# Three chunks of an input projection by seven half-size products instead of eight

## The chip, the core and the metric

The kernel runs on one core of one Trainium2 chip. The metric is device time in microseconds, the median of repeated executions. One further execution was profiled. In the profile the engines are PE (TensorE matmuls), PEld (TensorE weight loads), DVE (VectorE), ACT (ScalarE), POOL (GpSimd) and SP (the queue that issues most DMAs); a name like SPq is an engine's instruction queue.

## What is computed

One layer in float32 for 256 tokens of width 1024: RMSNorm, one input projection whose columns are split among the inputs of two token mixers, the mixers, an output projection with residual, and a mixture of 32 experts. Cut to what matters:

```python
h = rms_norm(x, norm1_gain[layer])
proj = jnp.einsum('bsd,dn->bsn', h, w_in[layer])
q_a, k_a, v_a, q_i, k_i, w_i, q_b, k_b, v_b, g_b = jnp.split(proj, cuts, axis=-1)
...
out_a = dsa_attention(q_a, k_a, v_a, q_i, k_i, w_i, rel_bias, topk)   # indexer: relu(q_i k_i), weighted by w_i, top 64 keys
q_b = rotary(q_b.reshape(bsz, s, B_HEADS, B_QK_DIM), pos)
k_b = rotary(k_b.reshape(bsz, s, B_HEADS, B_QK_DIM), pos)
y_b = retention(q_b, k_b, v_b)
...
out_b = jax.nn.silu(g_b) * y_b
x = x + jnp.einsum('bsm,md->bsd', jnp.concatenate([out_a, out_b], -1), w_out[layer])
x = x + moe_ffn(rms_norm(x, norm2_gain[layer]), ...)                  # 32 experts, top 4
```

## The kernel before

The kernel is written for five engines by hand; each engine's block lists its instructions in order, and semaphores order the engines among each other. The normalised activations lie transposed in `hT`: 8 slices of 128 contraction rows by 256 tokens, not yet scaled by the tokens' inverse norms (`st[:, 6:8]`). The projection is worked in chunks of 512 columns, `C_QI, C_QKB, C_VB, C_GB, C_QA, C_KA, C_VA`, each a 1024 x 512 block of weights in one of four SBUF slots `win[0..3]`; SP loads the first four at the start and each later one when its slot is free (`load_win`, L251).

A chunk by token (`by_token`, `one_tile`, L1123 to L1132) takes, for each of two tiles of 128 tokens, 8 products of a 128x128 weight load with 512 moving columns, summed in one PSUM bank. `C_QKB` has the same products written out at L1193, with `index_scores` of the indexer put between them; `C_VB` and `C_GB` go through `chunk` (L1142). `C_QA` and `C_KA` go `by_head` (L1134), with 256 moving columns a product. A float32 product is two MATMUL records in the trace.

The order on TensorE around the change is: the index queries, `C_QKB` into banks 0 and 1 with four groups of index scores (banks 4 to 7), `C_VB` into banks 2 and 3, a wait for `rotated`, eight transposes of the rotated q and k (L1204), one product for the row of inverse norms (L1207), `C_GB` into banks 0 and 1, the retention scores (L1214, L1216) into banks 4 to 7, `C_QA`, the retention values, `C_KA`.

ScalarE takes the chunks out of PSUM and scales them by the inverse norms in the same instruction (L520 for q and k, L526 for the values), takes the relu of the index scores (L517), and the exponential of the gate (L540). VectorE adds the eight index heads into `score` (L770, L772; each an addition of two SBUF tensors with a factor), finds the top 64 keys by eight rounds of maxima and replacements (L781 to L788), splits the bias table into parts (L797, L799), finishes the gate (L807 to L809), and multiplies the retention scores by the decay (L814). GpSimd issues small table loads, multiplies q and k by the rotation table (`rot`, L459, four operations) and combines them (L463, L464), which releases `rotated`; later it loads the relative bias (L469, L470) and adds the mask (L476).

The relu of group 2 and 3 waits for `idx_added`, since `relu` has two buffers. The expert part begins behind the output projection and the router and streams 403 MB of expert weights (32 experts of 1024 x 2048 and 1024 x 1024 float32) through two SBUF rings; its loads are issued by SP as products free the rows.

Of the kernel before, what the change touches and what calls it, by code (L numbers as in the profile page):

```python
# [75 lines left out]
def hybrid_block(nc, x, norm1_gain, w_in, rel_bias, idx_k_ln_gain, idx_k_ln_bias, ret_gn_gain, w_out,  # L76
# [3 lines left out]
    with ctx:  # L80
# [24 lines left out]
        one_ready = sem("one_ready"); zeros_ready = sem("zeros_ready")  # L105
# [37 lines left out]
        va = carve(high, 5632, [TT, 512])  # L143

# [41 lines left out]
        x_in = [sem(f"x_in{t}") for t in range(TT)]; cols_sb = sem("cols_sb"); small_in = sem("small_in"); rel_in = sem("rel_in"); gain_in = sem("gain_in"); ln_in = sem("ln_in"); rot_in = sem("rot_in")  # L186
        wki_in = sem("wki_in"); dec_in = sem("dec_in"); br_in = sem("br_in"); gq_in = sem("gq_in"); rank_in = sem("rank_in"); wr_in = sem("wr_in"); late_consts = sem("late_consts")
# [17 lines left out]
        vb_sb = sem("vb_sb"); g_exp = sem("g_exp"); g_silu = sem("g_silu")  # L205
# [39 lines left out]
        C_QI, C_QKB, C_VB, C_GB, C_QA, C_KA, C_VA = range(7)  # L245
        CHUNK_COL = (1536, 2120, 2632, 3144, 0, 512, 1024)
# [187 lines left out]
        @block.gpsimd  # L434
        def _(pool):
            chain = [0]

            def link(ins):
                chain[0] += 1
                ins.then_inc(pool_chain, 1)  # L440
                pool.wait_ge(pool_chain, chain[0])


            for half in (slice(0, 64), slice(64, 128)):
                pool.dma_start(ln_rows[0:1, half], idx_k_ln_gain).then_inc(ln_in, 16)
                pool.dma_start(ln_rows[1:2, half], idx_k_ln_bias).then_inc(ln_in, 16)
            pool.dma_start(onehot[0:32, :], c_onehot).then_inc(rel_in, 16)
            pool.dma_start(relb[0:32, :], rel_bias).then_inc(rel_in, 16)
            pool.dma_start(rot, c_rot.rearrange("p (a t n) -> p a t n", a=2, t=TT)).then_inc(rot_in, 16)
            pool.wait_ge(win_in[C_QKB], 16)  # L450
            pool.dma_start(br[:, :], b_router.to_broadcast((P, NE))).then_inc(br_in, 16)
            pool.dma_start(gain_q, norm2_gain[0].rearrange("(c q j) -> q c j", c=2, q=P)).then_inc(gq_in, 16)
            pool.wait_ge(qkb_sb, 2)
            pool.wait_ge(rot_in, 16)
# [26 lines left out]
        def _(act):  # L481
# [7 lines left out]
            act.wait_ge(one_ready, 2)  # L489
# [219 lines left out]
        def _(dve):  # L709
# [9 lines left out]
            v.memset(zeros, 0.0).then_inc(zeros_ready, 1)  # L719
# [19 lines left out]
            ins.then_inc(diag_ready, 1)  # L739

# [16 lines left out]
            link(v.tensor_copy(cols[:, 20:22], ps[:, 4, 400:402]))  # L757

# [3 lines left out]
            v.tensor_scalar(kiT, ps[:, 5, 0:S], cols[:, LNG:LNG + 1], cols[:, LNB:LNB + 1], ALU.mult, ALU.add).then_inc(kiT_sb, 1)  # L762

# [11 lines left out]

            link(v.memset(score[0:64, P - CH:P], NEG))
# [27 lines left out]

            for t in range(TT):
# [3 lines left out]
                v.scalar_tensor_tensor(gb[:, t, :], ps[:, t, :], st[:, 6 + t:7 + t], gb[:, t, :], ALU.mult, ALU.mult).then_inc(g_silu, 1)  # L809

            dve.wait_ge(dec_in, 16)
            for h in range(BH):
                dve.wait_ge(ret_s, h // 2 + 1)
                v.tensor_tensor(sT[:, h, :], ps[:, 4 + h, 0:KW], dec[:, h, :], ALU.mult).then_inc(sT_sb, 1)  # L814
# [100 lines left out]
            dve.wait_ge(br_in, 16)  # L915
# [182 lines left out]
        def _(pe):  # L1098
# [3 lines left out]
            pe.wait_ge(zeros_ready, 1)  # L1102
# [26 lines left out]
            def by_token(w, bank, n):  # L1129
                for t in range(TT):  # L1130
                    ins = one_tile(w, bank, n, t)
                return ins  # L1132

# [8 lines left out]
            def chunk(c, banks, form):  # L1142
                pe.wait_ge(win_in[c % 4], 16 * (c // 4 + 1))
                ins = form(win[c % 4], banks) if form is by_head else form(win[c % 4], banks, 512)
                ins.then_inc(proj_done, 1)
# [8 lines left out]
            for k in range(KD):  # L1154
# [4 lines left out]
                if k == 3:  # L1159
                    pe.wait_ge(rel_in, 32)  # L1160
                    pe.wait_ge(ln_in, 64)
# [26 lines left out]

            pe.wait_ge(kiw_sb, 2)
            pe.wait_ge(win_in[C_QKB], 16)  # L1190
            for t in range(TT):
                for k in range(KD):
                    ins = mm(ps[:, t, :], hT[:, k, P * t:P * t + P], win[C_QKB][:, k, :], start=(k == 0), stop=(k == KD - 1))  # L1193
                    if k % 4 == 1:
                        index_scores(2 * t + k // 4)
            ins.then_inc(proj_done, 1)
            chunk(C_VB, 2, by_token)
            pe.wait_ge(rotated, 2)
            pe.wait_ge(idx_relu, 4)
            for which in range(2):  # L1200
                for g in range(2):
                    for t in range(TT):
                        at = 256 * which + 128 * g
                        ins = nc.tensor.transpose(ps[:, 4 + which, S * g + P * t:S * g + P * t + P], qkb[:, t, at:at + 128], ident)  # L1204
                ins.then_inc(qkbT_tr, 1)
            pe.wait_ge(diag_ready, 1)
            mm(ps[:, 6, 0:S], ones_early, diag.rearrange("p t n -> p (t n)"), start=True, stop=True).then_inc(row_mm, 1)  # L1207
            pe.wait_ge(qkb_sb, 2)
            chunk(C_GB, 0, by_token)
            pe.wait_ge(qkbT_sb, 2)  # L1210
            pe.wait_ge(row_sb, 1)
# [6 lines left out]
            pe.wait_ge(vb_sb, 2)  # L1218
# [9 lines left out]
            pe.wait_ge(g_silu, 2)  # L1228
# [404 lines left out]
```

## Time and profile before

| what | value |
| --- | --- |
| median of 3 runs | 1078.7 us (1077.63 to 1080.11) |
| the profiled execution | 1080.09 us |
| its span, first to last instruction | 1078.3 us |
| busy PE, DVE, ACT, POOL | 1040.4, 265.9, 152.9, 22.2 us |
| mean granted TensorE clock | 0.986 of 2.4 GHz |
| DMA | 429.87 MB, mean 399 GB/s |

The chain that ended last is followed back from the last instruction: at each step to what released it, or to the instruction before it on its engine. Granted clock is a share of 2.4 GHz, so 0.5 is the 1.2 GHz level. A DMA's time to landing runs from its issue. PE's records overlap, since matmuls are pipelined; in the chain they are cut to their own share of the time.

### The profile page before, as it was taken

How to read it: one execution, taken by the hardware profiler on the slowest of the kernel's cores; microseconds unless marked ns; L12 is line 12 of the kernel's file. 1: busy time of each engine (PE TensorE's matmuls, PEld its weight loads, DVE VectorE, ACT ScalarE, POOL GpSimd, SP SyncE). 2: the span in 40 equal slices, each digit the busy share in tenths (PEclk: the TensorE clock that was granted, in tenths of full speed). 3: DMA queues.
4: the chain of work that ended last, by engine and by line, in shares of the span. 5: the costliest groups of instructions: out<-in, count | busy, mean ns of one | idle time of the engine just before them, and what ended most of it. 6: DMA issues, size and time to landing. Idle time of an engine off the chain costs nothing.

```text
span 1078.3 us, 11417 instructions
## 1 busy us (share of the span) xinstructions
PE 1040.4 (96%) x4628; PEld 399.4 (37%) x4628; DVE 265.9 (25%) x649; ACT 152.9 (14%) x278; POOL 22.2 (2%) x29
## 2 busy tenths in 40 slices
PE   9999999999999999999999999898989899999996
PEld 7458454333333333333333333232323233333331
DVE  2455622422222222222220302121222212120221
ACT  1231322110111110101010111011101101111111
POOL 1212000000000000000000000000000000000000
PEclk9999998999999999999998999999999999999999
DMA  9886957999999999999999999999999999999996
GB/s 330 239 245 269 378 217 266 423 428 421 428 433 430 430 430 430 430 430 432 432 430 430 430 432 433 432 429 434 432 433 432 430 434 430 435 423 434 425 422 246
DMA packets 35376, 429.87 MB, mean 399 GB/s; under 512 B 5164, under 2 KB 6608, under 8 KB 16624
## 3 DMA queue, kind: packets, MB, share of 16 engines
q1 hardware_dynamic: 33424, 426.03, 93.8%
q10 hardware_dynamic: 1216, 1.70, 1.1%
q0 software_dynamic: 704, 1.71, 0.6%
q8 instruction: 21, 0.34, 0.1%
q14 instruction: 11, 0.09, 0.0%
HBM read 426.80 MB, written 2.62 MB: 398 GB/s over the span
## 4 chain that ended last, share of the span: by engine, by line
PE 72%; DMA 26%; SPq 0%; DVE 0%; issue 0%; ACT 0%; DVEq 0%
PE ps L1399 30%; DMA w1r<-w_mlp 24%; PE ps L1429 13%; PE ps L1467 5%; PE ps L1376 4%; PE ps L1126 3%; PE ps L1138 3%; DMA w2r<-w_mlp 2%; PE ps L1193 1%; PE ps L1257 1%; PE ps L1302 1%; PE ps L1158 1%; PE ps L1268 1%; PE ps L1383 1%; PE ps L1407 1%; PE ps L1443 1%
## 5 line engine op out<-in xcount | busy, mean ns | idle before, releaser
L1399 PE MATMUL ps<-w1r,arena 128*64 128x512 f32 x2024 | 478.0, 608 | 21.0 <-DMA w1r<-w_mlp 21.0
L1399 PEld LDWEIGHTS ps<-w1r,arena 128*64 128x64 f32 x2024 | 138.2, 139 | 281.7 <-issue 253.6
L1429 PE MATMUL ps<-w2r,arena 128*64 128x512 f32 x960 | 211.4, 593 | 6.6 <-DMA w2r<-w_mlp 6.6
L1429 PEld LDWEIGHTS ps<-w2r,arena 128*64 128x64 f32 x960 | 68.8, 137 | 145.1 <-issue 135.5
L964 DVE TENSOR_TENSOR arena<-ps,cols 128x512 f32<-128x512 f32 x31 | 21.4, 692 | 277.0 <-PE ps L1383 277.0
L1002 DVE TENSOR_TENSOR arena<-arena 128x512 f32<-128x512 f32 x32 | 22.1, 692 | 163.8 <-ACT arena L618 163.7
L985 DVE TENSOR_SCALAR arena<-small,rank,gate 128x64 f32<-128x64 f32 x128 | 31.3, 308 | 121.4 <-PE ps L1487 121.4
L622 ACT ACTIVATE arena<-ps 128x512 f32<-128x512 f32 x31 | 18.5, 597 | 290.0 <-PE ps L1407 290.0
L1376 PE MATMUL ps<-acc,arena 128*64 128x512 f32 x248 | 58.6, 592 | 0.0
L1467 PE MATMUL ps<-arena 128*128 128x512 f32 x112 | 55.5, 618 | 0.0
L627 ACT ACTIVATE arena<-ps 64x512 f32<-64x512 f32 x29 | 17.1, 591 | 268.2 <-PE ps L1429 268.2
L611 ACT ACTIVATE arena<-ps 128x512 f32<-128x512 f32 x31 | 18.5, 597 | 155.0 <-PE ps L1376 155.0
L996 DVE TENSOR_SCALAR arena<-ps 128x512 f32<-128x512 f32 x32 | 33.5, 1047 | 20.7 <-PE ps L1399 20.7
L997 DVE TENSOR_SCALAR arena<-ps 128x512 f32<-128x512 f32 x32 | 33.8, 1057 | 0.0
L1467 PEld LDWEIGHTS ps<-arena 128*128 128x128 f32 x112 | 19.0, 189 | 36.0 <-issue 36.0
L1376 PEld LDWEIGHTS ps<-acc,arena 128*64 128x64 f32 x248 | 18.1, 137 | 35.1 <-issue 35.1
L955 DVE TENSOR_SCALAR sel_z<-small 96x64 bf16 (+1 forms) x30 | 5.7, 190 | 101.6 <-PE ps L1399 101.6
L1138 PE MATMUL ps<-hx,w1r 128*128 128x256 f32 x128 | 28.1, 380 | 0.0
L1126 PE MATMUL ps<-w1r,hx 128*128 128x512 f32 x64 | 27.8, 592 | 0.0
L1138 PEld LDWEIGHTS ps<-hx,w1r 128*128 128x128 f32 x128 | 24.2, 190 | 3.3
L1407 PEld LDWEIGHTS ps<-small,arena 128*128 128x128 f32 x128 | 13.4, 140 | 26.0 <-issue 26.0
L999 DVE SCALAR_TENSOR_TENSOR arena<-arena 128x512 f32<-128x512 f32 x32 | 22.2, 692 | 1.1
(261 smaller groups left out, 591.4 us busy)
## 6 DMA issues: line engine op xcount, KB each, us to landing
w1r<-w_mlp SPq DMA_DIRECT2D x46, 4096.0 KB, 30.9
w2r<-w_mlp SPq DMA_DIRECT2D x29, 2048.0 KB, 17.5
w1r<-w_mlp SPq DMA_DIRECT2D x28, 2048.0 KB, 11.6
w2r<-w_mlp SPq DMA_DIRECT2D x14, 4096.0 KB, 21.1
w1r<-w_mlp SPq DMA_DIRECT2D x20, 1024.0 KB, 9.7
w1r<-w_in SPq DMA_DIRECT2D x6, 2048.0 KB, 19.5
w2r<-w_mlp SPq DMA_DIRECT2D x6, 1024.0 KB, 9.8
w1r<-w_out SPq DMA_DIRECT2D x2, 2048.0 KB, 13.4
```

The costliest lines, as they stand in the source:

```text
L985: ins = v.tensor_scalar(gated[:, t, which, at:at + 64], slotn, rank[:, t, bass.ds(e, 1)], gate[:, t, bass.ds(e, 1)], ALU.is_equal, ALU.mult)
L996: v.tensor_scalar(g3, z[:, :, :, 0], 7.0, None, ALU.min).then_inc(glu_ready, 1)
L997: v.tensor_scalar(l3, z[:, :, :, 1], 7.0, -7.0, ALU.min, ALU.max).then_inc(z_read, 1)
L999: v.scalar_tensor_tensor(lin, lin, 1.0, glu, ALU.add, ALU.mult).then_inc(prod_ready, 1)
L1002: v.tensor_tensor(lin, lin, sig, ALU.mult).then_inc(act_ready, 1)
L1126: ins = mm(ps[:, bank + t, 0:n], hT[:, k, P * t:P * t + P], w[:, k, 0:n], start=(k == 0), stop=(k == KD - 1))
L1138: ins = mm(ps[:, bank + g // 2, S * (g % 2):S * (g % 2) + S], w[:, k, P * g:P * g + P], hT[:, k, :], start=(k == 0), stop=(k == KD - 1))
L1376: ins = mm(ps[64 * c:64 * c + 64, 7, :], onehotP[:, par, t, :], acc[:, t, 512 * c:512 * c + 512], start=(t == 0), stop=(t == TT - 1))
L1399: ins = mm(ps[64 * c:64 * c + 64, z_bank(base, e) + n, :], hgT[:, par, k % 4, 64 * (k // 4):64 * (k // 4) + 64], cols_z, start=False, stop ...
L1407: ins = nc.tensor.transpose(ps[:, 7, P * j:P * j + P], lin[:, P * j:P * j + P], ident)
L1429: ins = mm(ps[at:at + 64, 6, :], actT[:, k % 4, 64 * (k // 4):64 * (k // 4) + 64], w2r[:, k // 2, col:col + 512], start=(k == 0), stop=(k ...
L1467: ins = mm(ps[:, 2 * t + c, :], gT[:, c, P * t:P * t + P], ysb[:, c, :], start=False, stop=False)
```

## The change

The 1024 x 512 weights of a chunk and the 256 x 1024 activations are each seen as 2 x 2 blocks, and the product of the blocks is formed from seven products of half-size blocks in place of eight (Winograd's form of Strassen's scheme). `C_QKB`, `C_VB` and `C_GB` are worked so.

- Four sums of activation blocks, `xsum`, are made once by VectorE behind `diag`.
- Three sums of weight blocks per chunk, `wsum`, and one that overwrites a block of the weights: for `C_QKB` by VectorE, ahead of its copy of the index queries; for `C_VB` and `C_GB` by GpSimd (`weight_sums`), ahead of the rotation.
- TensorE's `seven` forms the products, 256 columns each, two to a bank; the index scores stand behind products 0, 2, 4 and 5 of `C_QKB`. Its `ready` lists what a bank waits for. The banks are 0 to 3 for `C_QKB`, 4 to 7 for `C_VB`, and 3, 2, 0, 1 for `C_GB`.
- ScalarE takes only the first product out (`product_out`); VectorE adds the other six by seven additions (`joined`), each reading one SBUF and one PSUM operand: for q and k behind the index heads and ahead of the top-k, for the values between the two bias parts, for the gate behind `sel_z`.
- Results stay unscaled: VectorE scales the rotation table (four instructions ahead of the index heads), the decay product takes the factor (L814 becomes two instructions a head), the gate is finished from `g_raw` and moves behind the decay product.
- The wait for the gate ahead of `C_KA` goes; TensorE waits for the joined values ahead of the retention scores and for the joined gate ahead of `C_QA`. Some semaphores are merged to make room.

```diff
@@ GpSimd
+            def weight_sums(c):
+                w, (t2, t3, t4) = win[c], wsum[c - C_QKB]
+                b11, b12, b21, b22 = (w[:, k:k + 4, n:n + 256] for k in (0, 4) for n in (0, 256))
+                nc.gpsimd.tensor_tensor(t3, b22, b12, ALU.subtract).then_inc(w_sums, 1)
+                pool.wait_ge(w_sums, 4 * (c - C_VB) + 1)
+                nc.gpsimd.tensor_tensor(b12, b12, b11, ALU.subtract).then_inc(w_sums, 1)
...
+            pool.wait_ge(win_in[C_VB], 16)
+            weight_sums(C_VB)
+            pool.wait_ge(win_in[C_GB], 16)
+            weight_sums(C_GB)
+            pool.wait_ge(qkb_sb, 8)
+            pool.wait_ge(sums_scaled, 7)
@@ ScalarE
+            def product_out(to, c, banks, done):
+                act.wait_ge(products, 6 * (c - C_QKB) + 2)
+                nc.scalar.activation(to[:, 0, 0:256], ps[:, banks[0], 0:256], ACT.Copy).then_inc(done, 1)
@@ VectorE
+            dve.wait_ge(win_in[C_QKB], 16)
+            w, (t2, t3, t4) = win[C_QKB], wsum[0]
+            b11, b12, b21, b22 = (w[:, k:k + 4, n:n + 256] for k in (0, 4) for n in (0, 256))
+            for j, (to, a, b) in enumerate(((t3, b22, b12), (b12, b12, b11), (t2, b22, b12), (t4, t2, b21))):
+                v.tensor_tensor(to, a, b, ALU.subtract).then_inc(sums_scaled, 1)
+                dve.wait_ge(sums_scaled, j + 2)
...
+            dve.wait_ge(rot_in, 16)
+            for t in range(TT):
+                for which in range(2):
+                    ins = v.tensor_scalar(rot[:, which, t, :], rot[:, which, t, :], st[:, 6 + t:7 + t], None, ALU.mult)
+                ins.then_inc(sums_scaled, 1)
...
+            joined(qkb, C_QKB, QKB_BANKS, qkb_sb)
@@ TensorE
+            def seven(c, banks, sums, count, between=None, ready=None):
+                w, (t2, t3, t4) = win[c], wsum[c - C_QKB]
+                b11, b12, b21, b22 = (w[:, k:k + 4, n:n + 256] for k in (0, 4) for n in (0, 256))
+                a11, a12, a21, a22 = (hT[:, k:k + 4, n:n + P] for n in (0, P) for k in (0, 4))
+                s1, s2, s3, s4 = xsum
+                for i, (a, b, made) in enumerate(((a11, b11, 0), (a12, b21, 0), (s3, t3, 1), (s1, b12, 2), (s2, t2, 3), (a22, t4, 4), (s4, b22, 4))):
+                    if made:
+                        pe.wait_ge(sums, count + made)
+                    if ready is not None and i % 2 == 0 and ready[i // 2] is not None:
+                        pe.wait_ge(*ready[i // 2])
+                    for k in range(4):
+                        ins = mm(ps[:, banks[i // 2], 256 * (i % 2):256 * (i % 2) + 256], a[:, k, :], b[:, k, :], start=(k == 0), stop=(k == 3))
+                    ins.then_inc(products if i < 6 else proj_done, 1)
+                    if between is not None and i in between:
+                        index_scores(between.index(i))
...
-            chunk(C_VB, 2, by_token)
+            seven(C_QKB, QKB_BANKS, sums_scaled, 1, between=(0, 2, 4, 5))
+            pe.wait_ge(win_in[C_VB], 16)
+            seven(C_VB, VB_BANKS, w_sums, 0, ready=((idx_relu, 3), (idx_relu, 3), (idx_relu, 4), (idx_relu, 4)))
             pe.wait_ge(rotated, 2)
...
-            chunk(C_GB, 0, by_token)
+            seven(C_GB, GB_BANKS, w_sums, 4, ready=(None, (row_sb, 1), (qkbT_sb, 1), (qkbT_sb, 2)))
+            pe.wait_ge(vb_sb, 8)
```

Three places show how the instructions stand now. First GpSimd between its small loads and the rotation; `w2r` holds the rotation's buffers, `w1r` the chunks' weights and their sums, `win_in2` and `win_in3` are the landings of the value and gate weights. Before:

```order
L451 DMA gateT<-b_router 128x32 [waits win_in1]
L452 DMA gateT<-norm_gain 128x2x4
L459 ISA
L459 TENSOR_TENSOR w2r<-w2r 128x512 [waits rot_in,qkb_sb]
L459 TENSOR_TENSOR w2r<-w2r 128x512 [waits pool_chain] x3
L463 TENSOR_TENSOR w2r<-w2r 128x16x32 [waits pool_chain]
L464 TENSOR_TENSOR w2r<-w2r 128x16x32
```

And with the change:

```order
L463 TENSOR_TENSOR w1r<-w1r 128x1024 [waits win_in2]
L465 TENSOR_TENSOR w1r<-w1r 128x4x256 [waits w_sums]
L467 TENSOR_TENSOR w1r<-w1r 128x1024 [waits w_sums]
L469 TENSOR_TENSOR w1r<-w1r 128x1024 [waits w_sums]
L463 TENSOR_TENSOR w1r<-w1r 128x1024 [waits win_in3]
L465 TENSOR_TENSOR w1r<-w1r 128x4x256 [waits w_sums]
L467 TENSOR_TENSOR w1r<-w1r 128x1024 [waits w_sums]
L469 TENSOR_TENSOR w1r<-w1r 128x1024 [waits w_sums]
L481 TENSOR_TENSOR w2r<-w2r 128x512 [waits sums_scaled,qkb_sb]
L481 TENSOR_TENSOR w2r<-w2r 128x512 [waits pool_chain] x3
```

Eight sums of 128x1024 now stand ahead of the rotation on the same engine.

Second VectorE from the index queries' copy to the top-k; the sums are L792, the rotation table's scaling is L822, the index heads are L831 and L833 (L770 and L772 before), the join is L807 to L817. Before, the head of it:

```order
L760 COPY w2r<-ps 128x512 [waits proj_done,dve_chain]
L762 TENSOR_SCALAR arena<-ps,cols 128x256 [waits kiT_tr]
L770 TENSOR_SCALAR w2r<-w2r,arena 128x128 [waits idx_relu]
L770 TENSOR_SCALAR w2r<-w2r,arena 128x256
L772 SCALAR_TENSOR_TENSOR w2r<-w2r,arena 128x128 [waits idx_relu,idx_added]
L772 SCALAR_TENSOR_TENSOR w2r<-w2r,arena 128x256
```

And with the change, the head of it, and from its last index head on:

```order
L792 TENSOR_TENSOR w1r<-w1r 128x1024 [waits win_in1,dve_chain]
L792 TENSOR_TENSOR w1r<-w1r 128x4x256 [waits sums_scaled]
L792 TENSOR_TENSOR w1r<-w1r 128x1024 [waits sums_scaled] x2
L796 COPY w2r<-ps 128x512 [waits proj_done,sums_scaled]
L798 TENSOR_SCALAR arena<-ps,cols 128x256 [waits kiT_tr]
L822 TENSOR_SCALAR w2r<-w2r,st 128x32 [waits rot_in]
L822 TENSOR_SCALAR w2r<-w2r,st 128x32 x3
L831 TENSOR_SCALAR w2r<-w2r,arena 128x128 [waits idx_relu]
```

```order
L833 SCALAR_TENSOR_TENSOR w2r<-w2r,arena 128x128 [waits idx_relu,idx_added]
L833 SCALAR_TENSOR_TENSOR w2r<-w2r,arena 128x256
L807 TENSOR_TENSOR w2r<-w2r,ps 128x256 [waits qkb_sb,products,idx_added]
L808 TENSOR_TENSOR w2r<-w2r,ps 128x256
L810 TENSOR_TENSOR w2r<-w2r,ps 128x256 [waits qkb_sb]
```

The weights' sums moved in ahead of the copy, the scalings ahead of the heads, and the join, which `qkb_sb` counts for GpSimd, behind the heads.

## Rows read from the trace of the kernel before

**Rows 1.** The page: the chain that ended last, share of the span by engine
```profile
PE 72%; DMA 26%; SPq 0%; DVE 0%; issue 0%; ACT 0%; DVEq 0%
```

**Rows 2.** The chain in order of time, 0 to 205 us: start us, us, what
```profile
44.64 1.91 PE ps L1193 x4
...
46.56 13.73 PE ps L1126 x32
60.29 0.87 PE ps L1204 x8
...
61.60 13.73 PE ps L1126 x32
...
76.84 14.01 PE ps L1138 x64
```

**Rows 3.** Busy time by windows: us, PE, PEld, DVE, ACT, POOL busy, PEclk, DMA share, GB/s
```profile
200.00:400.00 200.00, 200.00 (x930) 68.40 (x929) 45.95 (x97) 23.98 (x41) 0.00 (x0) 1.00 1.01 428
```

**Rows 4.** Timeline of SP's queue, 105 to 205 us: start us, us, what
```profile
176.74 8.91 SPq L371 DMA_DIRECT2D w1r<-w_mlp  x6
```

**Rows 5.** Timeline of SP's queue, 3 to 20 us
```profile
6.08 4.66 SPq L254 DMA_DIRECT2D w1r<-w_in  x2
...
17.46 0.56 SPq L254 DMA_DIRECT2D w1r<-w_in  x1
```

**Rows 6.** DMA issues from 10.0 and from 17.3 us: KB each, median us to landing
```profile
w1r<-w_in SPq DMA_DIRECT2D x1, 2048.0 KB, 20.9
w1r<-w_in SPq DMA_DIRECT2D x1, 2048.0 KB, 18.0
```

**Rows 7.** Timeline of POOL, 0 to 110 us
```profile
22.09 0.54 POOL L451 DMA_DIRECT2D gateT<-b_router  x1 [17.15 <-DMA w1r<-w_in]
...
47.95 5.30 POOL L459 TENSOR_TENSOR w2r<-w2r 128x512 f32<-128x512 f32 x4 [24.60 <-ACT w2r L520]
...
54.55 1.27 POOL L464 TENSOR_TENSOR w2r<-w2r 128x512 f32<-128x512 f32 x1
...
82.14 7.68 POOL L476 TENSOR_TENSOR arena<-arena,w2r 128x384 f32<-128x384 f32 x8 [10.74 <-DMA arena<-rel_table]
```

**Rows 8.** POOL's groups by form: operands, count, busy us, mean ns, idle before
```profile
L476 POOL TENSOR_TENSOR arena<-arena,w2r 128x384 f32<-128x384 f32 x8 | 7.7, 994 | 10.7 <-DMA arena<-rel_table 10.7
L459 POOL TENSOR_TENSOR w2r<-w2r 128x512 f32<-128x512 f32 x4 | 5.1, 1266 | 24.8 <-ACT w2r L520 24.6
```

**Rows 9.** DVE's groups by form, 0 to 110 us
```profile
L729 DVE TENSOR_TENSOR hx<-ps,cols 128x512 f32<-128x512 f32 x4 | 2.5, 683 | 0.0
L797 DVE TENSOR_TENSOR arena<-arena,bias 32x2048 f32<-32x2048 f32 x1 | 2.3, 2280 | 0.0
L814 DVE TENSOR_TENSOR w1r<-ps,w1r 128x384 f32<-128x384 f32 x4 | 1.9, 548 | 0.0
L834 DVE TENSOR_TENSOR w1r<-w1r 128x512 f32<-128x512 f32 x2 | 1.4, 692 | 0.1
L807 DVE TENSOR_SCALAR w1r<-w1r 128x512 f32<-128x512 f32 x2 | 0.8, 421 | 8.7 <-ACT w1r L540 8.7
```

**Rows 10.** Timeline of DVE, 0 to 110 us
```profile
28.49 0.69 DVE L760 COPY w2r<-ps 128x512 f32<-128x512 f32 x1 [6.95 <-PE ps L1158]
...
45.60 1.53 DVE L772 SCALAR_TENSOR_TENSOR w2r<-w2r,arena 128x128 f32<-128x128 f32 x4 [2.96 <-ACT w2r L517]
...
54.90 0.41 DVE L788 MATCH_REPLACE8 w2r<-st,w2r 128x256 f32<-128x256 f32 x1
...
81.06 3.35 DVE L808 RECIPROCAL w1r<-w1r 128x512 f32<-128x512 f32 x1
...
85.11 1.94 DVE L814 TENSOR_TENSOR w1r<-ps,w1r 128x384 f32<-128x384 f32 x4
```

**Rows 11.** Busy time by windows, as in rows 3
```profile
564.00:568.00 4.00, 0.00 (x0) 0.00 (x0) 0.69 (x1) 1.24 (x3) 0.00 (x0) 0.86 0.99 426
568.00:572.00 4.00, 3.70 (x10) 1.24 (x12) 0.00 (x0) 0.00 (x0) 0.00 (x0) 0.50 1.03 442
572.00:576.00 4.00, 4.00 (x16) 1.18 (x15) 0.00 (x0) 0.00 (x0) 0.00 (x0) 0.79 0.93 401
```

More of the change, by code:

```diff
@@ L104, in hybrid_block @@
         spare = sb("spare", [P, 3])
-        one_ready = sem("one_ready"); zeros_ready = sem("zeros_ready")
+        one_ready = sem("one_ready"); products = sem("products")
         n_sweeps = sb("n_sweeps", [1, 1], I32)
@@ L143, in hybrid_block @@
         va = carve(high, 5632, [TT, 512])
+        xsum = [carve(high, at, [4, P]) for at in (2304, 2816, 3328, 7168)]
+        wsum = ([carve(low, at, [4, 256]) for at in (5120, 6144, 7168)],
+                [carve(high, at, [4, 256]) for at in (4096, 5120, 6144)],
+                [carve(high, 0, [4, 256]), carve(high, 1024, [4, 256]), carve(low, 1024, [4, 256])])
+        g_raw = yb
         mixT = carve(arena, 0, [KD, S])
@@ L739, in _ @@
             ins.then_inc(diag_ready, 1)
+            a11, a12, a21, a22 = (hT[:, k:k + 4, n:n + P] for n in (0, P) for k in (0, 4))
+            s1, s2, s3, s4 = xsum
+            link(v.tensor_tensor(s1, a21, a22, ALU.add))
+            v.tensor_tensor(s3, a11, a21, ALU.subtract)
+            link(v.tensor_tensor(s2, s1, a11, ALU.subtract))
+            v.tensor_tensor(s4, a12, s2, ALU.subtract).then_inc(sums_scaled, 1)
             dve.wait_ge(kiw_sb, 2)
@@ L762, in _, with joined @@
             v.tensor_scalar(kiT, ps[:, 5, 0:S], cols[:, LNG:LNG + 1], cols[:, LNB:LNB + 1], ALU.mult, ALU.add).then_inc(kiT_sb, 1)
+            def joined(to, c, banks, done):
+                c11, c12, c21, c22 = (to[:, t, n:n + 256] for t in range(TT) for n in (0, 256))
+                p2, p7, p5, p6, p4, p3 = (ps[:, banks[i // 2], 256 * (i % 2):256 * (i % 2) + 256] for i in range(1, 7))
+                base = 6 * (c - C_QKB)
+                dve.wait_ge(products, base + 6)
+                dve.wait_ge(done, 1)
+                v.tensor_tensor(c12, c11, p6, ALU.add).then_inc(done, 1)
+                v.tensor_tensor(c11, c11, p2, ALU.add).then_inc(done, 1)
+                dve.wait_ge(done, 2)
+                v.tensor_tensor(c21, c12, p7, ALU.add).then_inc(done, 1)
+                v.tensor_tensor(c12, c12, p5, ALU.add).then_inc(done, 1)
+                dve.wait_ge(done, 4)
+                v.tensor_tensor(c22, c21, p5, ALU.add).then_inc(done, 1)
+                v.tensor_tensor(c21, c21, p4, ALU.subtract).then_inc(done, 1)
+                dve.wait_ge(done, 5)
+                dve.wait_ge(proj_done, c + 2)
+                v.tensor_tensor(c12, c12, p3, ALU.add).then_inc(done, 1)
+            dve.wait_ge(rot_in, 16)
[3 more added lines that the diff above has]
+                ins.then_inc(sums_scaled, 1)
             for h in range(AH):
@@ L803, in _ @@
             ins.then_inc(late_consts, 1)
+            joined(g_raw, C_GB, GB_BANKS, gb_sb)
+            dve.wait_ge(dec_in, 16)
+            for h in range(BH):
+                dve.wait_ge(ret_s, h // 2 + 1)
+                v.scalar_tensor_tensor(sT[:, h, 0:S], ps[:, 4 + h, 0:S], st[:, 6:7], dec[:, h, 0:S], ALU.mult, ALU.mult)
+                v.scalar_tensor_tensor(sT[:, h, S:KW], ps[:, 4 + h, S:KW], st[:, 7:8], dec[:, h, S:KW], ALU.mult, ALU.mult).then_inc(sT_sb, 1)
             for t in range(TT):
@@ L808, in _ @@
                 link(v.reciprocal(gb[:, t, :], gb[:, t, :]))
[L809 to L814, printed above, removed]
+                link(v.scalar_tensor_tensor(gb[:, t, :], g_raw[:, t, :], st[:, 6 + t:7 + t], gb[:, t, :], ALU.mult, ALU.mult))
             dve.wait_ge(proj_done, 6)
@@ L1099, in _ @@
             mm = nc.tensor.matmul
-            pe.wait_ge(zeros_ready, 1)
+            pe.wait_ge(one_ready, 2)
             for i in range(5):
@@ L1127, in one_tile @@
                 return ins
[L1129 to L1132, printed above, removed]
             def by_head(w, bank):
@@ L1143, in chunk @@
                 pe.wait_ge(win_in[c % 4], 16 * (c // 4 + 1))
-                ins = form(win[c % 4], banks) if form is by_head else form(win[c % 4], banks, 512)
-                ins.then_inc(proj_done, 1)
+                form(win[c % 4], banks).then_inc(proj_done, 1)
             pe.wait_ge(wki_in, 16)
@@ L1203, in _ @@
                         at = 256 * which + 128 * g
[L1204 removed]
+                        ins = nc.tensor.transpose(ps[:, which, S * g + P * t:S * g + P * t + P], qkb[:, t, at:at + 128], ident)
                 ins.then_inc(qkbT_tr, 1)
             pe.wait_ge(diag_ready, 1)
[L1207 to L1211 removed]
+            mm(ps[:, 2, 0:S], ones_early, diag.rearrange("p t n -> p (t n)"), start=True, stop=True).then_inc(row_mm, 1)
+            pe.wait_ge(win_in[C_GB], 16)
+            seven(C_GB, GB_BANKS, w_sums, 4, ready=(None, (row_sb, 1), (qkbT_sb, 1), (qkbT_sb, 2)))
+            pe.wait_ge(vb_sb, 8)
             for g in range(2):
```

69 lines of the change are left out of this document (32 added, 37 removed).

## The prediction

> **What bounds the kernel now.** I read four views: the chain that ended last, the busy windows, the timelines of the engines around the projection, and the groups by form. By the page TensorE (PE) carries 72% of the chain and DMA 26% [rows 1]. In order of time these are two regimes. Up to 205 us the chain is PE work almost without a break: the rotated chunk (q and k of the retention heads) ends at 46.56, the value chunk takes the next 13.73, then come transposes, the gate chunk (13.73 again) and qa [rows 2]. Later the DMA engines set the pace: from 200 to 400 us their share is 1.01 at 428 GB/s [rows 3]. The stream of expert weights that runs from there to the end starts at 176.74, with loads that wait for PE's first expert step [rows 4]. So whatever moves PE before 176 moves the end one for one, in either direction.
>
> **TensorE.** A 128x512 chunk is 16 products of 512 columns, two records each: 32 records in 13.73 us [rows 2]. The new form has 7 x 4 products of 256 columns, 56 records. Of that shape qa has 64 records in 14.01, 0.219 each [rows 2]. 56 x 0.219 = 12.26, so a chunk gains 1.47, not the eighth (1.72) that the count of products promises. Three chunks gain **4.4 us**; the other end, with cost by columns alone, is 5.2. I take 4.4, since its row has the very shape. The index scores between the products are as many as before. The rotated chunk then ends at 45.1 and the value chunk at 57.35.
>
> **VectorE's new sums ahead of the rotated chunk.** Four of the activations, 128x512 from SBUF at 0.692 [rows 9], are 2.8 us at about 12 us, far ahead of the product that reads them. Four of the weights are 128x1024. Between 0.692 for 512 and 2.280 for 2048 [rows 9] a straight line gives 1.22, so 5 us with their waits. They start with the chunk's landing, which frees GpSimd (POOL) at 22.09 [rows 7], and end at 27.2. The copy of the index queries queued behind them runs at 28.49 [rows 10]: hidden, by 1.3 us. Without that cover the first index scores would slip one for one.
>
> **VectorE's joins.** Each chunk gets seven adds of 128x256 with one operand in PSUM. From 0.683 at 512 and 0.548 at 384 [rows 9] that is 0.41 each; partly overlapping, 2.7 a chunk. The rotated join stands behind the index heads, whose last four instructions end at 47.13 today [rows 10]. The last scores come 1.3 earlier now (one product of 1.75 ahead of 45.1; today at 44.64 [rows 2]), so the heads end at 45.8 and the join at 48.5, if nothing disturbs them. The join of the values ends long before the retention scores need its banks, and the gate's last add falls about a microsecond after its last product, under the first retention scores: I cost both at nothing. The top-k behind the rotated join slips about a microsecond, which the value and gate chunks hide. ScalarE loses work: three exits of 128x256 for six of 128x512.
>
> **Queues behind.** GpSimd's two small loads stay ahead of the sums. Behind the rotation it loads the relative bias and adds the mask, done at 89.82 today [rows 7]. With the top-k and the bias parts pushed back this may slip by some 8 us, to 98. VectorE needs it for the attention logits, behind qa and a second chunk of its length, after 104 (76.84 and twice 14.01 [rows 2]), and SP for two loads of expert weights that PE reads after 176 [rows 4]: nothing.
>
> **GpSimd.** Its operations take 0.994 for 128x384 and 1.266 for 128x512 [rows 8]: 2.354 for 128x1024 by the line. Eight, linked as the four that take 5.30 [rows 7], come to 19.3 us. The value weights are issued right after the rotated ones, at about 6.5 [rows 5], and land 20.9 later [rows 6], at 27.4. The gate weights follow at 17.46 + 18.0 = 35.5 [rows 5, 6], before the fifth sum. Alone, the sums end at 46.8, the rotation behind them starts with the join at 48.5, and its 7.87 (47.95 to 55.82 today [rows 7]) ends at 56.4. PE comes for it at 57.35: one microsecond to spare.
>
> **What decides: two engines in one stretch.** From 27.5 to 54 GpSimd would be busy all the time beside VectorE's four scalings of the rotation table and its eight index heads. The heads' additions and the scalings have only SBUF tensors as operands, two for an addition. The trace of before has no such pair: while GpSimd worked, VectorE ran maxima and replacements with one SBUF tensor, reciprocals, and products of PSUM with SBUF [rows 7, 10], and neither side slowed. The cost is therefore open between nothing and taking turns. I take the turns. VectorE adds two SBUF tensors in 0.692, as fast as PSUM with SBUF (0.683), and scales one SBUF tensor in 0.421 [rows 9]: in these two forms it draws nearly twice as much from SBUF in the same time as in any form that ran beside GpSimd, so rows of the latter say little about them. It is a choice, and the other end is the first rival.
> The Trainium skill, "SBUF — State Buffer", section "Who interferes with whom", states that a VectorE instruction with two SBUF inputs, or in a mode that uses both ports, contends with a GpSimd instruction that reads SBUF, and that the later one blocks until the first has finished. By that rule the sum is the 1083.9 below; read as if the rows of today held for every form, it is 1074.3. No run here shows it yet.
>
> **Taking turns, worked out.** Scalings 0.8 (an estimate: 0.2 each, half of the 0.421 at 512 [rows 9]), heads 8 x 0.765 = 6.1 (four instructions in 1.53 [rows 10]), sums 19.3: 26.2 from 27.5, to 53.7. The join ends at 56.4, the rotation at 64.3. PE has been waiting since 57.35: **6.9 us**. Part of it may come earlier instead, since the value chunk's first bank waits for a ScalarE exit that waits for the first heads; the end is the same. A wait of that length has a second price. In the expert part PE stood still over 564 to 568; the granted clock averaged 0.86 there, was 0.50 (the 1.2 GHz level) for the next 4 us, and came back inside 572 to 576, whose mean is 0.79 [rows 11]. That is 5.4 us at half speed after work resumed: **2.7 us** lost. Between nothing and 2.7 I take 2.7, the row being the nearest.
>
> **The sum.** -4.4 + 6.9 + 2.7 = **+5.2 us**. The profiled execution took 1080.1 us, the span of 1078.3 and 1.8 around it, so 1085.3 on its own count; it lies 1.4 above the median of the runs, 1078.7, to which the forecast is tied: **1083.9 us**.
>
> **Rivals.**
> 1. *No interference* (ends on the other side). The 1 us to spare holds and PE keeps all it saves: 1078.7 - 4.4 = **1074.3**. For it: no row shows either engine slowed by the other. Against it: no row has these operations together. It decides from the point where the rotation ends before 57.35. Chance 0.34.
> 2. *VectorE always goes first.* The heads then end as if alone; only GpSimd is pushed back, its sums to 53.7 and the rotation to 61.6. PE waits 4.2 and pays the clock: -4.4 + 4.2 + 2.7 = +2.5, **1081.2**. For it: VectorE's instructions stand nearly back to back, so GpSimd may find no gap. Chance 0.19.
> 3. *A draw.* Interference is partial; PE waits as long as it saves but too short for the clock, or the joins hold PE at the gate chunk: **1078.7**. Chance 0.10.
>
> **How the numbers follow.** The forecast has 0.37. A difference of about 0.2% (2.2 us) is what a measurement of this kernel can tell from none. Slower: all of the forecast's 0.37 and 0.15 of rival 2, together 0.52. Same: rival 3 and the rest of rival 2, 0.14. Faster: rival 1, 0.34. The likeliest case alone spans 1081.5 to 1085.5 (waits of 5.5 to 7.5, clock loss 0.5 to 2.7). Both signs hold much of the chance, so the range reaches from rival 1 with the larger saving, 1078.7 - 5.2 = 1073.5, to 1085.5.
>
> **What would show it.** Right: in the timeline of POOL the 128x1024 sums are spaced by more than 2.4 us, or VectorE's additions of 0.35 to 0.48 stretch to microseconds; PE's wait ahead of the eight transposes, none today, is 4 us or more, ended by GpSimd; the windows after it show a clock near 0.5. TensorE's 56 records a chunk take 12.3 busy us in any case. Wrong: sums done near 47 and transposes near 57.4, with no wait on PE; then the qa chunk starts at 72.4 and not 76.84 [rows 2], and the end moves by as much. A wait on the weights' sums or on the banks ahead of the retention scores would mean that I placed the price on the wrong wait.

## The result and the profile after

The changed kernel takes **1078.74 us** (median of 21 runs, 1077.20 to 1081.88), the kernel before beside it 1077.27 us (21 runs). The ratio is 1.0014, 95% interval 1.0009 to 1.002: slower by 1.5 us or 0.14%. That is inside the 0.2% that the prediction counted as the same, though 21 runs do tell it from nothing. The forecast was +5.2 us; the sign was right, the size was not. The time lies in the range.

The profiled execution took 1080.27 us, its span is 1078.5. GpSimd is busy for 41.9 us in place of 22.2, VectorE for 297.7 in place of 265.9, PE for 1031.1 in place of 1040.4.

POOL's timeline, where [rows 7] had only the two loads and the rotation (columns: start us, us, engine, line, operation, idle time before and what ended it):

```profile
27.12 2.35 POOL L463 TENSOR_TENSOR w1r<-w1r 128x1024 f32<-128x1024 f32 x1 [4.09 <-DMA w1r<-w_in]
...
34.41 2.48 POOL L469 TENSOR_TENSOR w1r<-w1r 128x1024 f32<-128x1024 f32 x1
36.84 2.40 POOL L463 TENSOR_TENSOR w1r<-w1r 128x1024 f32<-128x1024 f32 x1
...
44.23 2.41 POOL L469 TENSOR_TENSOR w1r<-w1r 128x1024 f32<-128x1024 f32 x1
52.84 5.31 POOL L481 TENSOR_TENSOR w2r<-w2r 128x512 f32<-128x512 f32 x4 [6.20 <-DVE w2r L817]
...
59.44 1.26 POOL L486 TENSOR_TENSOR w2r<-w2r 128x512 f32<-128x512 f32 x1
```

The eight sums run back to back from 27.12 to 46.64, and none is longer than 2.48. Then GpSimd stands idle for 6.20 us, until VectorE's join (L817) gives it q and k. The rotation ends at 60.70. VectorE's timeline over the same stretch says why the join was late:

```profile
27.58 0.69 DVE L796 COPY w2r<-ps 128x512 f32<-128x512 f32 x1 [1.00 <-PE ps L1216]
...
28.64 3.44 DVE L822 TENSOR_SCALAR w2r<-w2r,st 128x32 f32<-128x32 f32 x4
...
34.71 15.61 DVE L833 SCALAR_TENSOR_TENSOR w2r<-w2r,arena 128x128 f32<-128x128 f32 x14
50.35 0.42 DVE L807 TENSOR_TENSOR w2r<-w2r,ps 128x256 f32<-128x256 f32 x1
```

The copy, which reads PSUM, takes 0.69 as in [rows 10]. The four scalings of the rotation table take 3.44, and the fourteen head additions 15.61, or 1.1 each; in [rows 10] four of them took 1.53, 0.38 each. The chain of waits goes through these additions one by one (start us, us, what):

```profile
36.96 2.57 DVE w2r L833
39.53 0.03 issue
39.56 0.04 DVE w2r L833
39.59 2.21 issue
41.81 2.64 DVE w2r L833
...
49.06 0.49 DVE w2r L833
...
49.84 0.49 DVE w2r L833
```

Until GpSimd is done at 46.64, the chain moves in steps that end with its sums (at 36.9, 39.2, 41.7, 44.2 and 46.6); behind that, every addition is a matter of 0.4 us. In the 12 us before, over five sums, five additions got through; the other nine came after. PE's timeline shows who paid:

```profile
43.83 3.62 PE L1258 MATMUL ps<-w1r,hx 128*128 128x256 f32 x16
47.29 5.34 PE L1258 MATMUL ps<-w1r 128*128 128x256 f32 x24
52.47 1.89 PE L1258 MATMUL ps<-w1r,hx 128*128 128x256 f32 x8
...
60.75 1.97 PE L1274 MATMUL ps<-small,w2r 128*128 128x128 f32 x8 [4.67 <-POOL w2r L486]
...
63.37 5.26 PE L1258 MATMUL ps<-w1r,hx 128*128 128x256 f32 x16
...
78.69 1.56 PE L1197 MATMUL ps<-hx,w1r 128*128 128x256 f32 x6
```

PE waits 4.67 us for the rotation. The eight transposes behind the wait take 1.97, where the chain of before had 0.87 [rows 2], and the first sixteen records of the gate products 5.26, against 3.62 for the sixteen records at 43.83. The windows show the clock (us, then PE, PEld, DVE, ACT, POOL busy, then granted clock, DMA share, GB/s):

```profile
58.00:60.00 2.00, 0.00 (x0) 0.00 (x0) 1.93 (x9) 0.00 (x0) 1.92 (x3) 0.96 0.99 285
60.00:62.00 2.00, 1.25 (x6) 1.25 (x7) 1.97 (x11) 0.10 (x1) 0.70 (x1) 0.50 1.04 319
62.00:64.00 2.00, 2.00 (x8) 1.73 (x7) 1.90 (x11) 1.48 (x3) 0.00 (x0) 0.50 0.83 310
...
66.00:68.00 2.00, 2.00 (x9) 1.74 (x8) 1.97 (x7) 1.69 (x1) 0.00 (x0) 0.83 0.53 204
```

It fell to 0.50 (1.2 GHz) just before work resumed at 60.75 and rose again inside 66 to 68; the mean of 0.83 puts that at 66.7. So 5.9 us of work ran at half speed: 3.0 us lost, an estimate from these windows.

### The profile page after: what moved, and what is told of

Read it like the earlier page. It is cut to its first block, busy times and chain, and to the rows that moved or that the text cites. A ratio compares the mean times of both kernels' runs of the same rounds, so it can differ in the third digit from the quotient of the medians.

```text
span 1078.5 us, 11616 instructions
## 1 busy us (share of the span) xinstructions
PE 1031.1 (96%) x4700; PEld 412.6 (38%) x4700; DVE 297.7 (28%) x686; ACT 151.9 (14%) x277; POOL 41.9 (4%) x37
## 4 chain that ended last, share of the span: by engine, by line
PE 68%; DMA 27%; DVE 2%; issue 1%; POOL 1%; SPq 0%; ACT 0%; DVEq 0%
PE ps L1467 29%; DMA w1r<-w_mlp 25%; PE ps L1497 14%; PE ps L1535 5%; PE ps L1444 3%; PE ps L1197 3%; DMA w2r<-w_mlp 2%; PE ps L1325 1%; PE ps L1370 1%; PE ps L1216 1%; PE ps L1336 1%; PE ps L1258 1%; PE ps L1511 1%; PE ps L1451 1%; PE ps L1475 1%
## 5 line engine op out<-in xcount | busy, mean ns | idle before, releaser
L1467 PE MATMUL ps<-w1r,arena 128*64 128x512 f32 x2024 | 472.2, 602 | 20.4 <-DMA w1r<-w_mlp 20.3
L1066 DVE TENSOR_TENSOR arena<-arena 128x512 f32<-128x512 f32 x32 | 22.2, 692 | 170.4 <-ACT arena L642 170.3
L1475 PEld LDWEIGHTS ps<-small,arena 128*128 128x128 f32 x128 | 13.4, 140 | 26.0 <-issue 26.0
L1451 PEld LDWEIGHTS ps<-small,arena 128*128 128x128 f32 x124 | 13.0, 140 | 25.2 <-issue 25.2
L1063 DVE SCALAR_TENSOR_TENSOR arena<-arena 128x512 f32<-128x512 f32 x32 | 22.2, 692 | 1.1
```

The lines of the kernel that those rows point to most:

```text
L1063: v.scalar_tensor_tensor(lin, lin, 1.0, glu, ALU.add, ALU.mult).then_inc(prod_ready, 1)
L1066: v.tensor_tensor(lin, lin, sig, ALU.mult).then_inc(act_ready, 1)
L1451: ins = nc.tensor.transpose(ps[:, 7, P * j:P * j + P], hg[:, P * j:P * j + P], ident)
L1467: ins = mm(ps[64 * c:64 * c + 64, z_bank(base, e) + n, :], hgT[:, par, k % 4, 64 * (k // 4):64 * (k // 4) + 64], cols_z, start=False, stop ...
L1475: ins = nc.tensor.transpose(ps[:, 7, P * j:P * j + P], lin[:, P * j:P * j + P], ident)
```

## The experiments

The theory behind the first four: a scaling or a head addition of VectorE, whose operands all lie in SBUF, does not run while GpSimd works on a sum; PE's wait and its half clock follow from that alone. "After" means the changed kernel.

**Gate sums behind the rotation.** The two lines move down by some fifteen lines in GpSimd's block:

```diff
             weight_sums(C_VB)
-            pool.wait_ge(win_in[C_GB], 16)
-            weight_sums(C_GB)
             pool.wait_ge(qkb_sb, 8)
...
             nc.gpsimd.tensor_tensor(q4[:, :, 1, :], c4[:, :, 1, :], s4[:, :, 0, :], ALU.add).then_inc(rotated, 1)
+            pool.wait_ge(win_in[C_GB], 16)
+            weight_sums(C_GB)
```

> GpSimd makes the four gate sums behind its rotation in place of ahead of it; nothing else moves. Theory (each scaled table and each head step of VectorE waits out one GpSimd sum): the sums of the values end near 37, from there a head step takes 0.4 us again, VectorE is through its heads at about 45 and through the join at about 47.5, the rotation runs from 47.5 to 55.4, and TensorE, which ends its value chunk at 56.0, does not wait: its 4.67 us and the half clock behind them (3.0 us) go, and the attention's query chunk starts near 71 to 72 in place of 78.8. Time 5 to 7 us below the changed kernel, about 1072 to 1074. Rival A (the heads are slow for another reason, such as the relus of ScalarE): heads still end near 50, the wait stays above 4 us, time as the changed kernel's, 1078 to 1080. Rival B (the start is repaired but a later stage takes it back, as the transfers of the weights do not come earlier): the query chunk starts near 72 and the end comes less than 2 us earlier.

Measured: 1074.99 us, 0.9976 of the kernel before (0.9968 to 0.9985). The heads end at 45.5, the rotation at 55.9, and PE's wait and the half clock are gone, as the theory has it; the time is 1 us above what it gave. A new wait of 1.25 us, which was not expected, stands before the last gate products, on GpSimd's fourth gate sum, and the qa chunk starts at 72.92. This wait shows the same exclusion from the other side. PE's timeline, then POOL's:

```profile
67.74 1.99 PE L1258 MATMUL ps<-w1r,hx 128*128 128x256 f32 x8 [1.25 <-POOL w1r L469]
```

```profile
60.72 2.41 POOL L467 TENSOR_TENSOR w1r<-w1r 128x1024 f32<-128x1024 f32 x1
63.21 4.48 POOL L469 TENSOR_TENSOR w1r<-w1r 128x1024 f32<-128x1024 f32 x1
```

And VectorE's, in the same execution:

```profile
58.15 0.41 DVE L850 MATCH_REPLACE8 w2r<-st,w2r 128x256 f32<-128x256 f32 x1
58.60 2.12 DVE L853 TENSOR_SCALAR w2r<-w2r 128x128 f32<-128x128 f32 x1
...
60.84 2.31 DVE L857 COPY cols<-gateT 128x8 f32<-128x8 f32 x1
63.19 2.28 DVE L859 TENSOR_TENSOR arena<-arena,bias 32x2048 f32<-32x2048 f32 x1
65.50 0.42 DVE L807 TENSOR_TENSOR w1r<-w1r,ps 128x256 f32<-128x256 f32 x1
```

A copy of 8 elements took 2.31 us: it began 0.12 behind a sum and ended with it. At 63.19 VectorE was first by 0.02 us, and now its addition took the usual 2.28 [rows 9] while GpSimd's sum needed 4.48 in place of 2.35, 2.1 more. Whoever is first goes through and the other waits for the end. The replacement in the top-k (58.15, one tensor operand) and the join at 65.50 (one operand in PSUM) took what they take alone.

**Products in the place of the wait.** Ten products that nobody reads, so that PE does not stand still:

```diff
+            pe.wait_ge(qkb_sb, 8)
+            for i in range(10):
+                mm(ps[:, 3, 0:S], hT[:, i % KD, 0:P], hT[:, i % KD, :], start=True, stop=True)
             pe.wait_ge(rotated, 2)
```

> Ten products that nobody reads (some 4.4 us) on TensorE between the value chunk's products and its wait for the rotation; the rest is the changed kernel. Theory (the wait costs twice: its own 4.67 us, and about 3.0 us of half clock behind it): the rotation ends at 60.7 as before and TensorE goes on at the same time, but the granted clock stays at 1.00 from 60 to 68 and the query chunk starts about 3 us earlier, near 75.8; time 2 to 3 us below the changed kernel, near 1076. Rival A (the clock falls all the same, or the extra products end later than the rotation): query chunk within 1 us of 78.8, time within 1 us of the changed kernel. Rival B (later stages take it back): query chunk near 75.8, time within 1 us of the changed kernel.

Measured: 1077.13 us, 1.0002 of the kernel before (0.9993 to 1.0011). The rotation ends when it did, and the windows that had 0.50 after now read:

```profile
62.00:64.00 2.00, 2.00 (x11) 1.77 (x10) 1.94 (x10) 0.67 (x2) 0.00 (x0) 1.00 0.82 288
64.00:66.00 2.00, 2.00 (x11) 1.77 (x10) 2.00 (x1) 0.00 (x0) 0.00 (x0) 1.00 0.76 231
```

The qa chunk starts at 75.67 as the theory said, so the half clock is a price of its own, apart from the wait. Of the 3 us won there the medians show 1.6, the ratios 1.3. These runs spread over 4 us (1075.99 to 1080.02); whether the rest is scatter isn't settled.

**No sums on GpSimd.** The eight sums are left out, and the products read raw blocks of the weights, as many and as large, so the output is not the layer's:

```diff
-            pool.wait_ge(win_in[C_VB], 16)
-            weight_sums(C_VB)
-            pool.wait_ge(win_in[C_GB], 16)
-            weight_sums(C_GB)
...
+                if c != C_QKB:
+                    made_of = ((a11, b11, 0), (a12, b21, 0), (s3, b22, 0), (s1, b12, 0), (s2, b11, 0), (a22, b21, 0), (s4, b22, 0))
```

> Leaves out GpSimd's eight sums for values and gate; the products read raw blocks of the weights in their place, as many and as large, so outputs differ. Theory (VectorE waits out GpSimd's sums): the scaling of the tables falls from 0.86 and 1.34 to below 0.4 us each, a head step to about 0.4 us, heads end as soon as the last relu allows, near 42 to 44, the join is then set by the products of the chunk (43.9) and the rotation by the join, TensorE does not wait, time 5 to 8 us below the changed kernel. Rival A (the heads are slow by their own form or by ScalarE): head steps stay above 0.8 us and heads end near 50. If the time is more than 1 us below that of the kernel with late gate sums, the four sums that remain there still cost.

Measured: 1073.15 us, 0.9962 (0.9947 to 0.9976). VectorE's timeline:

```profile
29.05 0.67 DVE L818 TENSOR_SCALAR w2r<-w2r,st 128x32 f32<-128x32 f32 x4
31.58 0.55 DVE L827 TENSOR_SCALAR w2r<-w2r,arena 128x128 f32<-128x128 f32 x2 [1.86 <-ACT w2r L542]
...
36.15 1.53 DVE L829 SCALAR_TENSOR_TENSOR w2r<-w2r,arena 128x128 f32<-128x128 f32 x4 [3.25 <-ACT w2r L542]
...
43.87 1.53 DVE L829 SCALAR_TENSOR_TENSOR w2r<-w2r,arena 128x128 f32<-128x128 f32 x4 [1.68 <-ACT w2r L542]
```

The scalings fall from 3.44 to 0.67, an addition to 0.38, and VectorE waits for the relus again. The heads end at 45.4: later than expected (42 to 44), since the last relu itself comes at 43.9.

**Sums that only write.** Each of GpSimd's eight instructions fills its destination with a constant, so the output is not the layer's either:

```diff
-                nc.gpsimd.tensor_tensor(t3, b22, b12, ALU.subtract).then_inc(w_sums, 1)
+                nc.gpsimd.memset(t3, 0.03).then_inc(w_sums, 1)
```

> GpSimd's eight sums become fills of the same destinations with a constant, so GpSimd writes as much there and reads nothing; outputs differ. Theory 1 (VectorE's operation waits for any GpSimd operation that holds the buffer memory): scaled tables and head steps beside the fills still end only when a fill ends. Theory 2 (only operands read by both collide): beside the fills a head step takes 0.4 us and the scaling below 0.4 us, as without the sums. Either way the fills may be shorter than the sums (2.35 us): what counts is the mean of a head step whose time lies wholly beside fills.

One run: 1072.8 us. POOL's timeline, then VectorE's:

```profile
29.09 0.95 POOL L467 MEMSET w1r<- 128x1024 f32 x1
...
35.48 0.95 POOL L465 MEMSET w1r<- 128x1024 f32 x1
36.48 0.95 POOL L467 MEMSET w1r<- 128x1024 f32 x1
37.49 0.95 POOL L469 MEMSET w1r<- 128x1024 f32 x1
```

```profile
29.44 0.64 DVE L822 TENSOR_SCALAR w2r<-w2r,st 128x32 f32<-128x32 f32 x1
...
36.54 1.53 DVE L833 SCALAR_TENSOR_TENSOR w2r<-w2r,arena 128x128 f32<-128x128 f32 x4 [3.24 <-ACT w2r L546]
```

Four head additions stand beside the fills and take the 1.53 that they take alone: theory 2, for the additions. A fill does not hold them off and a sum does; the sum reads, but it is also another operation, and the two weren't told apart further. The scalings go by theory 1. The first one (29.44) ends at 30.08, just behind the fill that ends at 30.04, and took 0.64. The groups by form (count, busy us, mean ns) have the four beside the fills, then the four of the kernel without sums:

```profile
L822 DVE TENSOR_SCALAR w2r<-w2r,st 128x32 f32<-128x32 f32 x4 | 0.7, 457 | 0.0
L818 DVE TENSOR_SCALAR w2r<-w2r,st 128x32 f32<-128x32 f32 x4 | 0.7, 232 | 0.0
```

All four end within 0.1 us behind that fill, so their sum hardly shows it (0.71 from first to last, 0.67 without). That is one execution with one fill; but it says that a scaling waits even for an instruction of GpSimd that reads nothing.

**All sums on VectorE.** A version that follows from this: VectorE makes the eight sums while it waits for relus, and the last two behind the top-k.

```diff
             for h in range(AH):
+                weight_sum((1, 0, 2, 0, 2, 0, 1, 0)[h])
                 dve.wait_ge(idx_relu, h // 2 + 1)
...
             v.tensor_scalar(left[:, P:KW], left[:, P:KW], -3.2e38, MASKED, ALU.is_gt, ALU.mult).then_inc(mask_ready, 1)
+            weight_sum(2)
```

> All eight weight sums go to VectorE, into the times in which it waits for a relu (one ahead of head 0, two ahead of head 2, two ahead of head 4, one ahead of head 6) and two behind the top-k; GpSimd makes none. VectorE made such a sum in 1.25 us for the first chunk, and its gaps ahead of heads 0, 2, 4 and 6 without GpSimd's sums were 1.86, 3.25, 2.98 and 1.68 us. Theory (what costs is that the two engines exclude each other, not the sums as such): heads end near 45.5, the rotation starts near 48 and ends near 56, TensorE waits neither for it nor for a gate sum (the 1.25 us of the kernel with late gate sums goes), query chunk near 71.5, time as without the sums, 1072.5 to 1074. Rival A (VectorE's sums take longer beside the transfers, or the relus run behind, and the heads end after 46.5): rotation ends after 57, a wait of over 1 us, and the time is that of the kernel with late gate sums or above, 1075 or more.

Measured: **1073.02 us**, 0.9959 of the kernel before (0.9946 to 0.9973), the fastest version that leaves nothing out, ahead of both kernels. VectorE's timeline:

```profile
33.00 2.48 DVE L798 TENSOR_TENSOR w1r<-w1r 128x1024 f32<-128x1024 f32 x2
36.14 1.53 DVE L835 SCALAR_TENSOR_TENSOR w2r<-w2r,arena 128x128 f32<-128x128 f32 x4 [0.66 <-ACT w2r L531]
37.71 2.36 DVE L798 TENSOR_TENSOR w1r<-w1r 128x1024 f32<-128x1024 f32 x2
40.65 1.53 DVE L835 SCALAR_TENSOR_TENSOR w2r<-w2r,arena 128x128 f32<-128x128 f32 x4 [0.58 <-ACT w2r L531]
42.22 1.22 DVE L798 TENSOR_TENSOR w1r<-w1r 128x1024 f32<-128x1024 f32 x1
```

The sums lie in the gaps, with 0.6 us and more to spare in all but the last, the heads end at 44.96, and PE waits nowhere between 28 and 85 us.

**Both kernels once more.** Copies without an edit, for their profiles, because the windows of the first profile of before show a half clock far from the change:

```profile
168.00:170.00 2.00, 2.00 (x8) 0.60 (x6) 0.53 (x5) 0.60 (x3) 0.00 (x0) 0.50 0.97 418
170.00:172.00 2.00, 2.00 (x8) 0.56 (x10) 1.33 (x7) 0.00 (x0) 0.00 (x0) 0.50 0.97 410
```

> The kernel before once more, for its profile. Question: in its first profile the granted clock fell to 0.50 between 168 and 174, in the router's and gather's products, and in none of the five profiles of kernels with seven products. Theory 1 (chance of that one execution): the clock stays at 1.00 there, the expert step starts near 172 in place of 174.8, and the total is nearer to the median, 1077 to 1078. Theory 2 (it belongs to this kernel's order): the clock falls again at the same place and the expert step starts near 174.8; then the seven products won some 2.6 us there that the forecast did not count.

> The changed kernel once more, for its profile. Theory: what stands ahead of the experts is the same in every execution: GpSimd's sums end near 46.6, VectorE's heads near 50.3, TensorE waits 4.5 to 4.8 us for the rotation, the granted clock is 0.50 from 60 to 66, the query chunk starts within 0.5 us of 78.8 and the expert step near 174; what differs from execution to execution (1077.2 to 1081.9) lies in the experts. Rival: the wait or the half clock differ by more than 1 us, and with them the total.

Measured, one run each: 1078.21 and 1079.68 us. In the second profile of before the same windows read:

```profile
168.00:170.00 2.00, 1.77 (x12) 0.64 (x10) 1.42 (x10) 0.61 (x4) 0.00 (x0) 1.00 0.97 418
170.00:172.00 2.00, 1.95 (x13) 0.71 (x9) 0.58 (x4) 1.11 (x3) 0.00 (x0) 1.00 0.94 397
```

So that fall was a matter of the one execution, and it hid the loss: the two first profiles end within 0.2 us of each other (spans 1078.3 and 1078.5). In the second profile of after the wait and the half clock repeat. The wait is a little shorter than expected (4.21 for 4.5 to 4.8 us), the clock is 0.50 from about 59 to 66, and qa starts at 78.22, where 78.3 to 79.3 was expected. PE's timeline:

```profile
60.53 1.97 PE L1274 MATMUL ps<-small,w2r 128*128 128x128 f32 x8 [4.21 <-POOL w2r L486]
```

All nine profiles, in us (qa and the transposes of the rotated q and k from PE's timeline; the stream is SP's first load behind PE's first expert step, as in [rows 4]; "first" is the first product of the rotated chunk, "between" the time from it to qa):

| kernel | first | transposes | qa starts | between | stream starts | span | span less stream |
| --- | --- | --- | --- | --- | --- | --- | --- |
| before | 28.44 | 60.13 | 76.77 | 48.33 | 176.74 | 1078.3 | 901.6 |
| before, again | 28.29 | 59.97 | 76.61 | 48.32 | 174.34 | 1076.4 | 902.1 |
| after | 27.53 | 60.75 | 78.69 | 51.16 | 176.02 | 1078.5 | 902.5 |
| after, again | 27.78 | 60.53 | 78.22 | 50.44 | 175.54 | 1077.9 | 902.4 |
| gate sums behind | 28.00 | 56.39 | 72.92 | 44.92 | 170.24 | 1072.6 | 902.4 |
| products in the wait | 27.56 | 60.62 | 75.67 | 48.11 | 173.45 | 1074.5 | 901.1 |
| no sums | 27.94 | 56.33 | 71.32 | 43.38 | 170.04 | 1072.7 | 902.7 |
| only writes | 28.33 | 56.72 | 71.71 | 43.38 | 169.03 | 1071.0 | 902.0 |
| sums on VectorE | 28.00 | 56.38 | 71.38 | 43.38 | 168.71 | 1070.6 | 901.9 |

Three kernels without a wait share 43.38 to a hundredth. The products in the wait add 4.73 to it. The price of the half clock is read from the transposes to qa, where the wait is over: 15.0 us without a wait and 15.05 with products in its place, but 17.94 (after) and 17.69 (again), so 2.9 and 2.7. From the stream on, 902 us follow whatever came before, within a microsecond.

## Why the prediction was half right

**TensorE's gain (4.4): too small by half a microsecond.** 24 records of the value chunk lie between 47.29 and 52.47 in the profile of after, 0.216 each and not the 0.219 of qa; 43.38 against 48.32 is 4.9 for three chunks, between the 4.4 taken and the 5.2 of the other end.

**VectorE's sums for the rotated chunk: hidden,** as said. They run from 21.58 to 26.58, and the copy behind them waits another 1.00 for PE. **Joins:** 2.41 for the first, and no wait of PE on the other two. **GpSimd's sums alone:** 19.3 to 46.8 expected, 19.5 to 46.64 measured. The gate weights were in time for the fifth sum.

**Interference: right in kind, and this is the step that failed in size.** The sum of scalings 0.8, heads 6.1 and sums 19.3, from 27.5 to 53.7, adds up the durations of both engines, as if each instruction held off the other for its whole time in the timeline. What was shown: GpSimd loses next to nothing to a short addition of VectorE. Its five sums from 34.41 on lasted 2.34 to 2.48, against 2.35 undisturbed, although five additions of 0.38 went between. It kept its pace and ended at 46.64; only VectorE was held up. So the heads ended at 50.33 and not at 53.7, the rotation at 60.70 and not at 64.3, and the wait was 4.67 or 4.21 in place of 6.9, although PE itself came 1.3 earlier than forecast (56.08 for 57.35). Rival 2 ("VectorE always goes first") had a wait of 4.2 from the opposite order: near in number, wrong in mechanism. Of the signs named, the spacing of the sums by more than 2.4 says nothing: it is 2.43 for the first three too, which lasted their usual 2.35. The stretched additions, the wait ended by GpSimd and the clock near 0.5 came.
The Trainium skill, "SBUF — State Buffer", section "Who interferes with whom", has the exclusion: with two SBUF inputs against a GpSimd instruction that reads, not one that only writes, and the first comer has the shared ports for its whole instruction. The 2.57, the 4.48 against 2.35, and the 1.53 beside fills agree. The step from that rule to a sum of durations was mine. By the rule alone GpSimd's back-to-back sums hold VectorE for 2.4 us at a time, and the heads are the ones to fall behind.

**The clock (2.7):** right. 2.9 and 2.7 measured, and told apart from the wait by the ten products.

**One for one to the end:** right within a microsecond or so. From the stream on it holds by the last column of the table. Between qa and the stream lie 97.3 to 97.8 us, with two exceptions: 100.0 in the first profile of before, with its half clock, and 98.7 without sums, where PE waited 1.12 us for the output projection's weights.

The account, from the two "again" profiles: -4.9 for the products, +4.4 up to the transposes (the wait of 4.21 and 0.2 more around it) and +2.7 for the clock make the +2.1 from the first product to qa (50.44 less 48.32). The chunk began 0.5 earlier and 0.4 came back between qa and the stream; +1.2 is left at the stream (+1.7 by the other profile of after), where the medians differ by 1.5. Why the chunk begins earlier and what the 0.4 is wasn't tried. Rival 1, no interference, ends where the kernels without GpSimd sums or with all sums on VectorE end: 4.4 less than before was its forecast, 4.4 less was measured for the latter.

## What to carry to other kernels

Work that is handed to an idle GpSimd isn't free for VectorE: ask of each VectorE instruction beside it whether it takes two tensors from SBUF, or scales or copies one within SBUF. A long GpSimd instruction then stands in front of every short one of these kinds, while the short ones cost GpSimd little. Where VectorE has waits of its own, the same sums fit into those: 1.25 us there, 2.35 on GpSimd. And a wait on TensorE can cost more than its length: here 4.2 and 4.7 us cost another 2.7 and 2.9 for the half clock behind them.

## What the runs showed of the hardware

- A VectorE copy of 8 elements per partition took 2.31 us beside a GpSimd sum, 0.17 without. So instructions with one SBUF operand can be held up too, like the table scalings of 32 elements (up to 2.37 beside a sum, up to 0.64 beside a fill, 0.23 alone); maxima, replacements and instructions with a PSUM operand were not.
- The time that an instruction is listed with isn't the time for which it keeps the other engine out: an addition of 0.38 lengthened a sum by at most 0.13, while one of 2.28 lengthened it by 2.1. Nor do the listed starts decide to the hundredth who is first: an addition and a sum both stand at 41.81 in the profile of after, and the addition waited (2.63) while the sum took 2.34.
- The clock fell to 0.50 for some 6 us (168 to 174) in one of two executions of one kernel, where PE had last stood still for 0.2 us, as it had in the other: one profile can carry 2.2 us from qa to the stream (100.0 against 97.7) that another doesn't.
